# A two-layer block on one core: decayed queries made from the turned queries on VectorE, scalings on ScalarE, roots on GpSimd, and fewer transposes

## The reference

```python
# layer 1
xn = _rms(x, norm_w[l]);  h = xn @ w_in[l]
qa, ka, va, ga, qr, kr, vr, gr = jnp.split(h, offsets, axis=-1)
oa = _diff_attention(rms(qa), rms(ka), va, lam, slopes)       # 4 heads, two softmaxes each
oa = _rms(oa, subln_w[l]) * (1.0 - lambda_init)
# retention, 4 heads, chunks of 128 tokens; once forward, once backward over the tokens
inner = ((qc @ kc.T) * dmat) @ vc
cross = (qc * xi[..., None]) @ state                          # xi = exp(log_g * (n + 1))
state = chunk_decay * state + (kc * zeta[..., None]).T @ vc
orr = _rms(fwd + bwd)                                         # no weight
x = x + concat([oa * silu(ga), orr * silu(gr)]) @ w_out[l]
# layer 2
u = rms_norm(x, norm_g) @ w_in
v_c, b_c, c_c, z_c, q, k, v, z_a, gate_logits = jnp.split(u, SPLIT_POINTS, axis=-1)
y_a = (b_c * causal_depthwise_conv(c_c * v_c) * silu(z_c)) @ w_conv_out
y_b = (sliding_window_attention(rms(q), rms(k), v, sinks) * silu(z_a)) @ w_attn_out   # 16 heads on 4 key heads
x = x + (sigmoid(g_a) * y_a + sigmoid(g_b) * y_b) @ w_out
```

## Time and profile before

| | |
|---|---|
| Median of 3 runs | 814.11 us (814.0 to 814.99) |
| Profiled execution, span from first to last instruction | 811.6 us |
| Around the span, to the median | 2.5 us |
| Mean granted TensorE clock | 0.999 |
| TensorE busy | 805.4 us, 99% |
| VectorE busy | 634.0 us, 78% |
| ScalarE busy | 339.9 us, 42% |
| GpSimd busy | 187.8 us, 23% |

### The profile page before, as it was taken

One profiled execution on the slowest core, in us unless ns is written; L12 is line 12 of the kernel. 1 busy time (PEld: TensorE's weight loads), 2 busy tenths in 40 slices (PEclk: granted clock), 3 DMA queues, 4 the chain that ended last, 5 costly groups with the idle time before them and its releaser, 6 DMA issues.

```text
span 811.6 us, 11794 instructions
## 1 busy us (share of the span) xinstructions
PE 805.4 (99%) x4364; PEld 691.4 (85%) x4364; DVE 634.0 (78%) x1112; ACT 339.9 (42%) x721; POOL 187.8 (23%) x189
## 2 busy tenths in 40 slices
PE   9999999999999999999999999999999999999998
PEld 7788888888888888888888888888889988999986
DVE  5998778768984476885578788978798678599998
ACT  4374465632122254342545544551134222455580
POOL 2222111111121221122324555544260114000000
PEclk9999999999999999999999999999999999999999
DMA  7236644445143322336868677596935634866562
GB/s 241 88 96 233 233 155 156 151 161 182 53 156 114 95 78 78 90 93 130 177 144 163 140 151 161 131 182 135 202 104 183 182 98 135 235 184 183 184 203 78
DMA packets 132862, 120.47 MB, mean 148 GB/s; under 512 B 4749, under 2 KB 100550, under 8 KB 132806
## 3 DMA queue, kind: packets, MB, share of 16 engines
q1 hardware_dynamic: 124326, 102.94, 40.9%
q0 software_dynamic: 8448, 16.78, 12.4%
q10 hardware_dynamic: 32, 0.01, 0.0%
HBM read 117.62 MB, written 35.65 MB: 189 GB/s over the span
## 4 chain that ended last, share of the span: by engine, by line
PE 92%; DVE 5%; issue 1%; ACT 1%; DMA 1%; POOL 0%; DVEq 0%; ACTq 0%
PE proj L1886 23%; PE proj L1888 23%; PE proj L1887 23%; PE bank_t L1900 3%; PE bank_o L1975 2%; DVE x L1592 1%; PE score L1888 1%; PE score L1887 1%; PE score L1886 1%; DVE w_lo L1247 1%; PE score L2050 1%; PE score L1960 1%; PE score L1961 1%; PE score L2049 1%; PE bank_o L2068 1%
## 5 line engine op out<-in xcount | busy, mean ns | idle before, releaser
L1247 DVE TENSOR_TENSOR w_lo<-w_raw,w_hi 128x1024 fp32r<-128x1024 f32 x151 | 192.0, 1274 | 44.3 <-POOL w_hi L778 36.1
L778 POOL TENSOR_SCALAR w_hi<-w_raw 128x1024 fp32r<-128x1024 f32 x101 | 118.6, 1174 | 438.6 <-DMA w_raw<-in_w_in_dram 314.6
L1886 PE MATMUL proj<-xt_hi,w_hi 128*128 128x512 f32 (+1 forms) x448 | 171.2, 382 | 0.0
L1888 PE MATMUL proj<-xt_hi,w_lo 128*128 128x512 f32 (+1 forms) x448 | 168.1, 375 | 0.0
L1887 PE MATMUL proj<-xt_lo,w_hi 128*128 128x512 f32 (+1 forms) x448 | 167.8, 374 | 0.0
L1888 PEld LDWEIGHTS proj<-xt_hi,w_lo 128*128 128x128 f32 x448 | 84.4, 188 | 15.6
L1887 PEld LDWEIGHTS proj<-xt_lo,w_hi 128*128 128x128 f32 x448 | 84.5, 189 | 14.1
L1886 PEld LDWEIGHTS proj<-xt_hi,w_hi 128*128 128x128 f32 x448 | 84.5, 189 | 14.0
L1886 PE MATMUL proj<-w_hi,xt_hi 128*128 128x512 f32 x152 | 60.9, 401 | 0.2 <-ACT prob L1012 0.2
L1888 PE MATMUL proj<-w_hi,xt_lo 128*128 128x512 f32 x152 | 59.5, 391 | 0.0
L1887 PE MATMUL proj<-w_lo,xt_hi 128*128 128x512 f32 x152 | 59.4, 391 | 0.0
(11 more groups left out here) (471 smaller groups left out, 1871.2 us busy)
## 6 DMA issues: line engine op xcount, KB each, us to landing
w_raw<-in_w_in_dram SPq DMA_DIRECT2D x79, 512.0 KB, 3.8
w_sums<-in_w_in_dram SPq DMA_DIRECT2D x8, 1024.0 KB, 7.0
w_sums<-w_sums POOLq DMA_DIRECT2D x8, 1024.0 KB, 9.1
w_raw<-w_sums SPq DMA_DIRECT2D x16, 512.0 KB, 3.8
w_raw<-w_sums SPq DMA_DIRECT2D x32, 256.0 KB, 3.3
w_raw<-in_w_out_dram SPq DMA_DIRECT2D x14, 512.0 KB, 3.3
w_raw<-in_w_in_dram SPq DMA_DIRECT2D x26, 256.0 KB, 3.3
w_sums<-in_w_attn_out_dram SPq DMA_DIRECT2D x4, 1024.0 KB, 6.5
```

Of the source, the lines that this page charges most:

```text
L778: pool.tensor_scalar(hi, raw, 1.0, 1.0, ALU.mult, ALU.mult).then_inc(hi_done, 1)
L1247: dve.tensor_tensor(lo, raw, hi.bitcast(F32), ALU.subtract).then_inc(w_split, 1)
L1886: pe.matmul(out, left[0], right[0], start=first, stop=False)
L1888: return pe.matmul(out, left[1], right[0], start=False, stop=last)
```

## The change

The decayed queries are no longer made ahead of the transposes. The queries are turned as they are, and VectorE multiplies the turned queries, still in PSUM, by a table of decay factors along the tokens (`decays`, an exponential made once by ScalarE). So four of the eight `RT` blocks go, and the two `RN` steps of the queries. `RT`'s two pairs are listed ahead of `AV` of the same half. The retention's keys are copied by ScalarE once per head, with zeros in the half of the partitions that belongs to the other head (`rk_own`), and `RS` then runs on 128 rows. `KV`, `RS` and `RA` come one half earlier, the last two `F` two halves earlier. `ON` and the scaling of `RB` go from VectorE to ScalarE, four activations of 128x128 per head; the attention's roots are written to `rs_o` by VectorE's chain, the retention's are computed by GpSimd as a power of -0.5 (`retention_root`), called in the same loop that rounds the weights. `KT2` turns the keys once (`k_norm`), in two blocks that stand two halves apart, and ScalarE and VectorE each write a block in four pieces of 64 partitions. `RS_ROW` becomes four transposes of a broadcast column. `rows` is zeroed and transposed whole.

```diff
-RET_FIRST = DA_STEPS + 6
-RET_NORMS = (RET_FIRST + 3, RET_FIRST + 5, RET_FIRST + 9, RET_FIRST + 11)
+RET_FIRST = DA_STEPS + 5
+RET_NORMS = (RET_FIRST + 3, RET_FIRST + 5, RET_FIRST + 7, RET_FIRST + 9)
...
+    x = 2 * (g - DA_STEPS - 1)
+    if 0 <= x < 4:
+        out += [("RT", x), ("RT", x + 1)]
     if 3 <= g < DA_STEPS + 3:
         out.append(("AV", g - 3))
...
-    if g == DA_STEPS:
-        out += [("RN", 2), ("RN", 3)]
-    x = 2 * (g - DA_STEPS - 1)
-    if 0 <= x < 8:
-        out += [("RT", x), ("RT", x + 1)]
...
-    finals = {21: 0, 22: 1, 23: 2, 25: 3, 27: 4, 29: 5, 34: 6, 36: 7}
+    finals = {21: 0, 22: 1, 23: 2, 25: 3, 27: 4, 29: 5, 32: 6, 34: 7}
...
+            def retention_root(m):
...
+                pool.wait_ge(o_mean, m + 1)
+                pool.tensor_tensor(rs_o[:, DA_STEPS + ST * m:DA_STEPS + ST * m + ST], ret_mean[:, columns], minus_half[:], ALU.pow).then_inc(o_root, 1)
...
             def take_retention(m):
...
                 act.wait_ge(rt_done, m + 1)
-                if m == 6:
+                if m == 2:
                     act.wait_ge(av_done, DA_STEPS)
-                dst = rkT[:, m, :] if m < 2 else q_decT[:, m - 2, :] if m < 6 else rqT[:, m - 6, :]
-                act.activation(dst, score[:, m % 2, :], ACT.Copy).then_inc(rt_free, 1)
+                if m < 2:
+                    for c in range(2):
+                        last = act.activation(rk_own[:, 2 * m + c, :], score[:, m % 2, :], ACT.Copy, scale=half_of[:, c:c + 1])
+                else:
+                    last = act.activation(rqT[:, m - 2, :], score[:, m % 2, :], ACT.Copy)
+                last.then_inc(rt_free, 1)
...
+                        elif kind in ("ON", "RB"):
+                            h = m if kind == "ON" else DA_HEADS + m
+                            act.wait_ge(o_root, 1 if kind == "ON" else m + 2)
+                            for i in range(ST):
+                                o = o_raw[:, h % 4, i, :]
+                                last = act.activation(o, o, ACT.Copy, scale=rs_o[:, ST * h + i:ST * h + i + 1])
+                            last.then_inc(o_normed, 1)
...
+                    elif kind == "RT" and m >= 2:
...
+                        dve.wait_ge(rt_free, m + 1)
+                        for c in range(2):
+                            here, h = slice(c * HD, (c + 1) * HD), 2 * (m - 2) + c
+                            for d in range(2):
+                                last = dve.tensor_tensor(q_decT[d * HD:(d + 1) * HD, h, :].rearrange("p (s q) -> p s q", s=ST),
+                                                         score[here, m % 2, :].rearrange("p (s q) -> p s q", s=ST),
+                                                         decays[here, d, h, :].unsqueeze(1).broadcast_to([HD, ST, P]), ALU.mult)
+                        last.then_inc(q_decayed, 1)
...
-                    elif kind == "ON":
-                        o = o_raw[:, m, :, :]
-                        dve.tensor_tensor(o, o, rs_y[:, ST * m:ST * m + ST].unsqueeze(2).broadcast_to([P, ST, P]), ALU.mult).then_inc(o_normed, 1)
...
-                    pe.matmul(bank_o[:], ones, diag, start=True, stop=True).then_inc(rs_turned, 1)
+                    for s in range(ST):
+                        last = pe.transpose(bank_o[:, s * P:(s + 1) * P], rs_x[:, m, s:s + 1].broadcast_to([P, P]), ident[:])
+                    last.then_inc(rs_turned, 1)
...
-                        last = pe.matmul(score[:, 1, c * P:(c + 1) * P], rkT[r, m // 2, c * P:(c + 1) * P],
-                                         rqT[r, m // 2, c * P:(c + 1) * P], start=True, stop=True)
+                        last = pe.matmul(score[:, 1, c * P:(c + 1) * P], rk_own[:, m, c * P:(c + 1) * P],
+                                         rqT[:, m // 2, c * P:(c + 1) * P], start=True, stop=True)
```

More of the change, by code:

```diff
@@ L199, in steps_after @@
         out.append(("GATE", i // 2 - 1))
-    for kind, unit, first, later in TURNS:
-        j = 2 * (n - 4 * unit) + half - later
-        if 0 <= j < 4:
+    for kind, unit, first, later, count, apart in TURNS:
+        j, between = divmod(2 * (n - 4 * unit) + half - later, apart)
+        if between == 0 and 0 <= j < count:
             out.append((kind, first + j))
@@ L339, in build @@
         norm_rows = sb("norm_rows", [2 * KC, P], stack=start)
-        rows = sb("rows", [ROWS, P], stack=start); lam_v = sb("lam_v", [P, 4, HD], stack=start)
+        rows = sb("rows", [P, P], stack=start); lam_v = sb("lam_v", [P, 4, HD], stack=start)
         start.close()
@@ L346, in build @@
         scoring.close()
-        q_decay = sb("q_decay", [P, ST, RET_HEADS, 2, HD], stack=one)
+        rk_own = sb("rk_own", [P, RET_HEADS, S], stack=one)
         q_decT = sb("q_decT", [P, RET_HEADS, S], stack=one)
@@ L1162, in _ @@
                             act.wait_ge(t_done, T_USE[(kind, m)] + 1)
-                            act.activation(k2_hi[:, m, :], bank_t[:], ACT.Copy, scale=k2w).then_inc(qk2_hi_done, 1)
+                            for c in range(2):
+                                here = slice(c * HD, (c + 1) * HD)
+                                for r in halves(c):
+                                    last = act.activation(k2_hi[r, 2 * m + c, :], bank_t[here, :], ACT.Copy, scale=k2w[here, :])
+                                last.then_inc(qk2_hi_done, 1)
                         elif kind == "QT2":
@@ L1219, in done, with rsqrt @@
                 dve.wait_ge(dve_chain, chain[0])
-            def rsqrt(n, width):
+            def rsqrt(n, width, out=None, ready=None):
                 v, y, t = rs_v[:, 0:n], rs_y[:, 0:n], rs_t[:, 0:n]
@@ L1226, in rsqrt @@
                 done(dve.tensor_scalar(y.bitcast(I32), t.bitcast(I32), -1.0, float(RSQRT_SEED), ALU.mult, ALU.add))
-                for _ in range(3):
+                for i in range(3):
                     done(dve.scalar_tensor_tensor(out=t, in0=y, scalar=-0.5, in1=y, op0=ALU.mult, op1=ALU.mult))
                     done(dve.tensor_tensor(t, t, v, ALU.mult))
-                    done(dve.scalar_tensor_tensor(out=y, in0=t, scalar=1.5, in1=y, op0=ALU.add, op1=ALU.mult))
+                    if i == 2 and ready is not None:
+                        dve.scalar_tensor_tensor(out=out, in0=t, scalar=1.5, in1=y, op0=ALU.add, op1=ALU.mult).then_inc(ready, 1)
+                    else:
+                        done(dve.scalar_tensor_tensor(out=y, in0=t, scalar=1.5, in1=y, op0=ALU.add, op1=ALU.mult))
             def take_xt_low(m):
@@ L1306, in prepare_decays @@
                 minus_p = diff[:, CENTRE:CENTRE + 1]
-                for k, (sign, steps) in enumerate(((-1.0, 1.0), (1.0, P), (1.0, P - 1.0), (-1.0, 0.0))):
+                for c in range(2):
+                    here, there = halves(c)
+                    dve.memset(half_of[here, c:c + 1], 1.0).then_inc(halves_set, 1)
+                    dve.memset(half_of[there, c:c + 1], 0.0).then_inc(halves_set, 1)
+                for k, (sign, steps) in enumerate(((1.0, P - 1.0), (-1.0, 0.0))):
                     dve.tensor_scalar(steps_to[:, k:k + 1], minus_p, sign, float(steps), ALU.mult, ALU.add).then_inc(dve_chain, 1)
@@ L1943, in step @@
                     pe.wait_ge(xt_split, 5)
-                    pe.transpose(score[:, 0, 0:ROWS], rows[:], ident[0:ROWS, 0:ROWS]).then_inc(rows_turned, 1)
+                    pe.transpose(score[:, 0, 0:P], rows[:], ident[:]).then_inc(rows_turned, 1)
                 elif kind in ("KT", "QT"):
@@ L2032, in step @@
                     pe.wait_ge(heads_done, 3 * ST)
-                    transposes((kind, m), [k_dup[:, s, m * P:(m + 1) * P] for s in range(ST)], quarters(bank_t))
+                    transposes((kind, m), [k_norm[:, s, m * P:(m + 1) * P] for s in range(ST)], quarters(bank_t))
                 elif kind == "QT2":
```

110 lines of the change are left out of this document (58 added, 52 removed).

## The result

The changed kernel takes 818.56 us (median of 20 runs, 817.9 to 819.21), the kernel before in the same session 814.69; the ratio is 1.0042, with a 95% interval from 1.0031 to 1.0053. It is slower by some 3.4 to 3.9 us, where the forecast was 1.0 and no measurable change. The profiled spans are 816.2 and 811.6, 4.6 apart.

A forecast was written before the change was run, and what follows sets the result against it. TensorE, busy 805.4 of 811.6 us, was taken as the bound; −4.4 of work, +3.6 of wait for F0 and +1.8 for F1 made +1.0 us: span 812.6, time 815.1, range 811.0 to 816.9.

The forecast's parts named there:

- F0: TensorE's transposes of the first normalised attention head: they would wait 3.6 us for their late source.
- The removed work: Work leaving TensorE through fewer RT and KT2 transposes, RS_ROW and RS on 128 rows: 4.4 us less.
- The multiplies: VectorE's eight multiplies of the turned queries ahead of the reduce: 0.70 us each, 5.6 in all.
- the stretched small operation: A tiny operation of VectorE's root chain, slowed beside GpSimd's w_hi: 0 or 0.72 us, taken as 0.3.
- Rival 1: The waits on TensorE stay small, below 2.8 us in all, so faster: 809.7 to 812.4; chance 0.16.
- rival 2: Each transpose taken from TensorE is worth its full duration, 3.9 us more gained: 811.2; chance 0.05.
- The rest: Constant work, removed multiplies, KT2's pieces and GpSimd's four roots at 0.5 us each: all put at nothing.
- The 6 us to spare: Slack found everywhere from F1 on, nearest at KV2's bank: 9.5 us of TensorE against 3.1 of VectorE.
- Rival 4: GpSimd's root is slow, 3.3 us each: 817.9, deciding from 2.2 us a root; chance 0.07.
- F1: TensorE's next F block waits 1.8 us for the bank that VectorE's F0 product frees.
- Rival 3: TensorE's clock falls in the pause before F0, up to 2.7 us more behind it: 816.0; chance 0.18.
- KT2: ScalarE's four operations of 0.69 us instead of one for layer 2's keys: nothing, at most 2.1 us.

The follow-up runs named there:

- no_decay_products: The changed kernel without the eight multiplies, the decayed queries set to zero earlier while VectorE is idle; 813.78 us, ratio 0.9991 to the kernel before.
- multiplies_early: The changed kernel with VectorE multiplying the queries once turned and ScalarE copying them afterwards; 816.16 us, ratio 1.0017 to the kernel before.
- root_behind: The changed kernel with GpSimd's root of a head called behind the rounding of the same weight piece; 816.74 us, ratio 1.0024 to the kernel before.
- pause_filled: The changed kernel with 17 unread matmuls ahead of TensorE's wait for F0; 820.68 us, ratio 1.0071 to the kernel before.
- all_three_old_keys: The changed kernel with multiplies_early, root_behind and order_alone, but layer 2's keys written twice and turned in four blocks; 810.94 us, ratio 0.9957 to the kernel before.
- order_alone: The changed kernel with the first head scaled ahead of the tanh and F0's product ahead of the first retention state; 820.02 us, ratio 1.0067.

## Why the prediction was wrong

The steps up to F0 held. The removed work was worth 4.8 us for the 4.4 forecast: a pair of RT blocks gave 0.91 for 0.87, an RS behind F0 0.39 for 0.34, and ROWS, put at nothing, 0.28. The multiplies took 5.62 for 5.6. F0 waited 3.95 for 3.6; the stretched small operation cost 0.48 where 0.3 was put in, and the rest is smaller differences along the chain. no_decay_products and multiplies_early show by experiment that the multiplies make F0 late. Rival 1, small waits, is out, as is rival 2.

On the two pages drawn on: sixteen transposes fewer gave 1.82 us, 0.114 each with the start of the projections behind them, near the step of 0.109. The Trainium skill's "TensorE: Matmul & The Clock Gate", section "Part 4: PE-mode transpose", gives about 275 ns for one in a kernel; the saving here does not go by that duration. The eight multiplies on alternating halves run without overlap, at 0.70 each. The Trainium skill's "VectorE: DVE Perf Modes", section "Two Vector instructions with no wait between them", has such instructions held until the earlier ones are finished, and the trace agrees.

**The step that failed** is in "The rest", on GpSimd: "Twice, before the last KV, 1.6 each is 3.2 us of the 6 to spare: nothing." The mechanism, a rounding queued behind a root, was right. Four things in it were not. The root took 1.04 us for 0.5, and VectorE stood still for 2.2 to 2.6 at a head, not 1.6. There were four roots, not two, since the retention norms go on behind the last KV. The 6 us to spare counted 3.1 of VectorE's work, for KV1 and RS1; its whole list from head to head keeps it busy for 7.49, which leaves 2.0 of TensorE's 9.5, less than it now stood still at a head. And the first customer to suffer was not KV2's bank but the last gate tile, whose evacuation on VectorE the output projection awaits; the forecast followed the steps' banks alone, not the projection's. It cost 1.84 us by the starts of the matmuls, and root_behind gave the same 1.84 back. Rival 4 named this loss and put its threshold at a root of 2.2 us; it decided at 1.04.

**F1** was mis-sized: 1.8 forecast, 2.64 measured. VectorE's list from the tanh on took 6.73 (183.90 to 190.63) for 6.2, the first gate product taking 1.13 instead of 0.6 beside GpSimd's w_hi. The rest is TensorE at the low clock, which comes to F1 0.3 behind VectorE. Rival 3's clock fell as it said, but its price, 0.9 beyond the wait, was too high: by pause_filled F1 could have come no more than 0.2 to 0.3 earlier with the full clock.

**KT2** was "nothing, at most … 2.1" and gave back 0.59, by all_three_old_keys all of its 0.88. This lay inside the bounds, but the sum had it at nothing; why the places behind KT2 are late is open.

The spans differ by 4.6 us where the sum said 1.0: 0.35 at F0, 0.84 at F1, 1.84 at the gate tile and 0.59 behind KT2 were missing, 3.6 in all. The 0.4 saved beyond the count and the 0.4 of small steps elsewhere cancel, which is luck. The medians differ by 3.9.

## What to carry to other kernels

Count, for an engine that does not look like the bound, what a full turn of its loop takes with the new links in it (here mean, root, rounding, low part: 10.0 us a head against 9.5 of TensorE), and not whether one step has slack; and look for its customers also among the evacuations that no step names. A link that two engines hand to and fro belongs behind work that the other one waits for in any case. And a fix may show nothing, or a loss, until the wait behind it is gone as well: order_alone lost 1.5 us by itself, since its gain became a longer pause with a low clock behind it, and gave 3.4 with the roots out of the way.

## What the runs showed of the hardware

A power of 128x4 on GpSimd took 1.02 to 1.04 us in the change, where VectorE stood still beside it, and 1.88 to 1.93 in root_behind, where VectorE's w_lo ran. There w_lo ends at 203.17 and the root, begun at 202.19, at 204.07, 0.90 behind it; the other three roots end 0.88 to 0.89 behind their w_lo. The other way round, GpSimd's w_hi ends at 179.00 in the change and VectorE's small operation, begun at 178.38, at 179.03; another w_hi ends at 184.52 and the gate product beside it at 185.06; in the earlier trace rows the ends are 204.57 and 204.58. In all these rows the operation that began second ends as if it had waited for the first one's end. No run was made to try this.

The granted clock fell to 0.50 behind the pause of 3.95 us in the change, and behind 4.6 in order_alone. Behind a pause of 2.25 us it was 1.00 in multiplies_early and 0.64 on the mean in pause_filled, where the pause came after 17 extra matmuls and a full half. So the length of a pause alone doesn't tell. What else does is open.
